# A second merge planned up to 48 gathers earlier, and routing's table lookup in bfloat16

## The reference, cut to what matters

```python
merged = sigmoid(g_a) * (y_a @ w_branch_a) + sigmoid(g_b) * (y_b @ w_branch_b)
h = layer_norm(ALPHA * x + merged @ w_out, ln1_g, ln1_b)
# peer(h): product-key retrieval, 8 heads x top 16 of 128 x 128 experts
q = (h @ w_q).reshape(N, 8, 2, 128)
s = einsum('thcd,chkd->thck', q, sub_keys)           # two half scores of 128 keys
sv, si = top_k(s, 16)
cand = sv[:, :, 0, :, None] + sv[:, :, 1, None, :]   # 16 x 16 candidates
cidx = si[:, :, 0, :, None] * 128 + si[:, :, 1, None, :]
top, j = top_k(cand.reshape(N, 8, 256), 16)
experts = take_along_axis(cidx.reshape(N, 8, 256), j)
gate = softmax(top)
pre = einsum('thkd,td->thk', expert_u[experts], h)
f = einsum('thk,thkd->td', gate * gelu(pre), expert_v[experts])
x = layer_norm(ALPHA * h + f, ln2_g, ln2_b)
```

## Time and profile before

| | |
|---|---|
| median of three runs | 2483.57 us (2473.17 to 2494.70) |
| the profiled execution | 2469.11 us |
| its span, first to last instruction | 2467.3 us |
| mean granted TensorE clock | 0.862 |
| busy share PE, DVE, ACT, POOL | 73%, 58%, 13%, 53% |
| read from memory | 783.86 MB |

### The profile page before, as it was taken

How to read it: one execution, slowest core, us unless ns; L and a number is a source line. 1 busy time by engine, 2 the same in 40 slices (tenths; PEclk the granted TensorE clock), 3 DMA queues, 4 the chain that set the end, 5 groups by cost and what they waited for, 6 DMA issues and landing times. The chain is left out here.

```text
span 2467.3 us, 23559 instructions
## 1 busy us (share of the span) xinstructions
PE 1810.1 (73%) x7247; PEld 762.4 (31%) x7247; DVE 1434.7 (58%) x3191; ACT 309.9 (13%) x737; POOL 1299.2 (53%) x1175
## 2 busy tenths in 40 slices
PE   9999998889779656565576667677778985555466
PEld 6767645645344212111121111221123341110011
DVE  2115875897745843999755669855334447434400
ACT  0214442101010100101010100111010010000000
POOL 1100000467645574545655557767766656767764
PEclk9998987999889888877888889999988996766788
DMA  4206331989979898999999999999999999999997
GB/s 185 71 3 197 95 95 36 336 322 406 409 260 374 290 356 307 402 394 387 392 400 388 402 377 368 370 348 381 393 366 409 409 396 364 376 369 378 354 380 291
DMA packets 259505, 791.67 MB, mean 321 GB/s; under 512 B 31506, under 2 KB 56147, under 8 KB 258803
## 3 DMA queue, kind: packets, MB, share of 16 engines
q0 software_dynamic: 166400, 604.58, 64.3%
q1 hardware_dynamic: 91124, 180.56, 20.8%
q10 hardware_dynamic: 1856, 5.03, 0.5%
HBM read 783.86 MB, written 5.59 MB: 320 GB/s over the span
## 5 line engine op out<-in xcount | busy, mean ns | idle before, releaser
L1319 PE MATMUL ps<-arena 128*32 128x512 f32 x2304 | 790.2, 718 | 346.5 <-DMA arena<-peer_v,arena 295.5
L2001 DVE CUSTOM_DVE_ANT_0 arena<-arena 128x1024 f32<-128x1024 f32 x576 | 695.3, 1226 | 563.5 <-DMA arena<-peer_u,arena 499.7
L895 POOL DMA_INDIRECT arena<-peer_u,arena x576 | 662.0, 1149 | 355.8 <-issue 160.7
L895 POOL DMA_INDIRECT arena<-peer_v,arena x576 | 616.9, 1071 | 393.5 <-PE ps L1319 186.8
L1319 PEld LDWEIGHTS ps<-arena 128*32 128x32 f32 x2304 | 156.7, 122 | 890.3 <-issue 641.3
L1114 PE MATMUL ps<-arena 128*128 128x448 f32 (+2 forms) x512 | 159.2, 472 | 21.3 <-DVE arena L1887 13.2
L1152 PE MATMUL ps<-arena 128*128 128x128 f32 (+2 forms) x768 | 150.4, 354 | 2.3 <-ACT arena L1504 2.3
L1275 PE MATMUL ps<-arena 128*64 128x512 f32 (+1 forms) x512 | 95.5, 516 | 69.3 <-DMA arena<-v_b 66.7
L877 POOL MEMSET arena<- 128x1024 f32 x1 | 1.0, 953 | 274.2 <-ACTq L701 274.2
L927 PE MATMUL ps<-arena 128*128 128x296 f32 (+1 forms) x512 | 130.9, 416 | 6.0 <-DMA arena<-xT 6.0
L1152 PEld LDWEIGHTS ps<-arena 128*128 128x128 f32 x768 | 108.4, 196 | 49.7 <-issue 17.0
(11 more groups left out here) (195 smaller groups left out, 1674.8 us busy)
## 6 DMA issues: line engine op xcount, KB each, us to landing
arena<-k_b SPq DMA_DIRECT2D x128, 256.0 KB
arena<-v_b SPq DMA_DIRECT2D x128, 256.0 KB
arena<-w_mix SPq DMA_DIRECT2D x56, 512.0 KB
arena<-w_q SPq DMA_DIRECT2D x48, 512.0 KB
arena<-kv_a SPq DMA_DIRECT2D x128, 128.0 KB
arena<-w_out SPq DMA_DIRECT2D x24, 512.0 KB
arena<-peer_u,arena POOLq DMA_INDIRECT x576
arena<-peer_v,arena POOLq DMA_INDIRECT x576
```

The costliest lines, as they stand in the source:

```text
L895: pool.indirect_dma_start(out=rows[slot_of[n]], out_offset=None, in_=io["peer_v"] if v else io["peer_u"], in_offset=bass.IndirectOffsetOnA ...
L1319: last = pe.matmul(bank(6 + a, 512, 32 * lane, 32 * lane + 32), strips[:, GT * (G % 2) + k % GT, MID - r_:MID - r_ + 32], rows[slot_of[n]] ...
L2001: dve.tensor_tensor_reduce(out=row, in0=row, in1=h, scale=1.0, scalar=0.0, op0=ALU.mult, op1=ALU.add, accum_out=pre[:, k:k + 1]).then_inc( ...
```

## The change

Three numbers of the plan and its gaps change, tile 1's routes get a running position, and the lookup of step 3 is written anew:

```diff
-        ALONE = 48
+        ALONE = 32
...
             if p:
-                out += [(("mix", p, 0), (0, 10, 6)[p])]
+                out += [(("mix", p, 0), (0, 7, 6)[p])]
                 for m in range(1, KD):
-                    out += [(("mix", p, m), (0, 3, 1)[p]), (("mixed", p, m - 1), (0, 7, 3)[p])]
+                    out += [(("mix", p, m), (0, 2, 1)[p]), (("mixed", p, m - 1), (0, 5, 3)[p])]
                 out += [(("mixed", p, KD - 1), 1)]
-                out += [(("out", p, k), (0, 4, 2)[p]) for k in range(KD)]
+                out += [(("out", p, k), (0, 3, 2)[p]) for k in range(KD)]
...
-                out.append((("query", p, m), (2, 4, 1)[p]))
+                out.append((("query", p, m), (2, 3, 1)[p]))
...
+        at = 0
         for g in range(4):
+            at = max(at, where["score", 1, g] + 2)
             for s_ in range(4):
-                put(where["score", 1, g] + 2 + 3 * s_, "route", 1, g, s_)
+                put(at, "route", 1, g, s_)
+                at += 3
...
-                lagging(dve.tensor_copy(siF[0:nt], si[0:nt]))
-                step(dve.tensor_scalar(jbits[0:nt], tj[0:nt], 4, None, ALU.logical_shift_right))
-                step(dve.tensor_copy(ja[0:nt], jbits[0:nt]))
-                step(dve.tensor_scalar(jbits[0:nt], tj[0:nt], 15, None, ALU.bitwise_and))
-                step(dve.tensor_copy(jb[0:nt], jbits[0:nt]))
-                for c, (jx, ex) in enumerate(((ja, e0), (jb, e1))):
-                    o = oh[0:nt]
-                    o4 = o.rearrange("p (h k) a -> p h k a", h=2)
-                    step(dve.tensor_tensor(o, jx[0:nt].rearrange("p h k -> p (h k)")[:, :, None].to_broadcast([nt, 32, PK]),
-                                           const("iota16", nt)[:, None, :].to_broadcast([nt, 32, PK]), ALU.is_equal))
-                    step(dve.tensor_tensor(o4, o4, siF4[0:nt, :, c, None, :].to_broadcast([nt, 2, PK, PK]), ALU.mult))
-                    step(dve.tensor_reduce(ex[0:nt].rearrange("p h k -> p (h k)"), o, AX_X, ALU.add))
...
+                lagging(dve.tensor_copy(si_b[0:nt], si[0:nt]))
+                for c, (op, by) in enumerate(((ALU.logical_shift_right, 4), (ALU.bitwise_and, 15))):
+                    step(dve.tensor_scalar(jbits[0:nt], tj[0:nt], by, None, op))
+                    step(dve.tensor_copy(j_b[0:nt, c, :], jbits[0:nt].rearrange("p h k -> p (h k)")))
+                o = oh[0:nt]
+                step(dve.tensor_tensor(o, j_b[0:nt, :, :, None].to_broadcast([nt, 2, 32, PK]),
+                                       iota_b[0:nt, None, None, :].to_broadcast([nt, 2, 32, PK]), ALU.is_equal))
+                o5 = o.rearrange("p c (h k) a -> p c h k a", h=2)
+                for c in range(2):
+                    lagging(dve.tensor_tensor(o5[:, c], o5[:, c], si4[0:nt, c, :, None, :].to_broadcast([nt, 2, PK, PK]),
+                                                     ALU.mult))
+                dve.wait_ge(dve_seq, done[0])
+                step(dve.tensor_reduce(e01[0:nt].rearrange("p c n -> p (c n)"), o.rearrange("p c n a -> p (c n) a"), AX_X, ALU.add))
```

More of the change, by code:

```diff
@@ L259, in program @@
         SCB = (0, 1, 2, 0, 1)
-        cand, oh = r.take(2, PK * PK), r.take(32, PK)
+        cand, oh = r.take(2, PK * PK), r.take(512).bitcast(BF16).rearrange("p (c n a) -> p c n a", c=2, a=PK)
         sv = r.take(4, PK)
         si = r.take(4, PK).bitcast(U32)
-        siF = r.take(4, PK)
-        ja, jb, e0, e1 = (r.take(2, PK) for _ in range(4))
+        si_b, j_b = (r.take(2 * PK).bitcast(BF16).rearrange("p (c a) -> p c a", a=n) for n in (PK, 2 * PK))
+        iota_b, e01 = r.take(PK // 2).bitcast(BF16), r.take(2, 2 * PK)
         tj = r.take(2, PK).bitcast(U32)
@@ L1925, in route @@
                 sv4 = sv.rearrange("p (h c) a -> p h c a", c=2)
-                siF4 = siF.rearrange("p (h c) a -> p h c a", c=2)
+                si4 = si_b.rearrange("p (h c) a -> p c h a", c=2)
                 h0, h1 = 2 * g, 2 * g + 2
@@ L1947, in route @@
-                dve.scalar_tensor_tensor(ids[i % 2][0:nt, 32 * g:32 * g + 32], e0[0:nt].rearrange("p h k -> p (h k)"), 128.0,
-                                         e1[0:nt].rearrange("p h k -> p (h k)"), ALU.mult, ALU.add).then_inc(pair_routed, 1)
+                lagging(dve.tensor_copy(si_b[0:nt], si[0:nt]))
+                for c, (op, by) in enumerate(((ALU.logical_shift_right, 4), (ALU.bitwise_and, 15))):
+                    step(dve.tensor_scalar(jbits[0:nt], tj[0:nt], by, None, op))
+                    step(dve.tensor_copy(j_b[0:nt, c, :], jbits[0:nt].rearrange("p h k -> p (h k)")))
@@ L1950, in gate_in @@
+                dve.wait_ge(dve_seq, done[0])
+                step(dve.tensor_reduce(e01[0:nt].rearrange("p c n -> p (c n)"), o.rearrange("p c n a -> p (c n) a"), AX_X, ALU.add))
+                dve.scalar_tensor_tensor(ids[i % 2][0:nt, 32 * g:32 * g + 32], e01[0:nt, 0, :], 128.0, e01[0:nt, 1, :],
+                                         ALU.mult, ALU.add).then_inc(pair_routed, 1)
             def gate_in(i):
@@ L2017, in _ @@
             end_phase(dve, 2)
+            step(dve.tensor_copy(iota_b, const("iota16")))
             for kind, *at in plan:
```

## The result

The median went from 2478.37 us (2463.70 to 2494.70, four executions) to 2534.66 us (2531.34 to 2540.05, four): the ratio is 1.0227, with a 95% interval from 1.0158 to 1.0297. The kernel is slower, by 56 us instead of the 27 that were forecast, and the time lies above the range. The profiled execution took 2540.05 us, 70.9 more than that of before.

The account below looks back on a forecast made before the run. PE was taken to bound the second merge, SP's issues the stage behind it, and DMA the late stretch. Terms -34 + 68 - 6 - 1 = +27 us on a level of 2480.1 gave 2507 us (+1.1%), range 2460 to 2530.

Parts of the forecast that it names:

- the mixes were PE's: Second merge's mixes: PE sets their pace, so they end at about 610 us instead of 617.1.
- the wait at `coef_t`: Tile 0's coefficients in the second merge: PE waits some 13 us for VectorE, a wait the change adds.
- The term of -34: Second merge: its last score comes at about 796 us instead of 829.7, 34 us earlier.
- a gather left for the end costs its full time: Late stretch, where DMA is full: 48 more gathers at 1.42 us each add 68 us.
- The rival that they ride in holes: Late gathers are not the limit, so the merge's 34 us last to the end: about 2440 us; chance 0.15.
- the rival of the long wait at `coef_t`: PE waits 25 us rather than 13 and the mixes give nothing: +49, 2529 us; chance 0.08.
- It stays 114.6: Last score to `ix` of chunk 1: length set by SP's 112.1 us of `kidx` issues, unchanged at 114.6 us.
- I cost this at nothing: SP covers it: Behind the merge: PE reaches `ix` 1 earlier and waits longer for `kidx`, at a cost of 0.
- I take 6 us back, between 0 and 20: Middle, 1500 to 1660 us at 356 GB/s: moved cache loads fill DMA there and save 6 us.
- 1 more for the lookup: Four lookups in tile 3's routes save 3 us of DVE, of which 1 us is taken.
- My last rival: DVE held the mixes: 72 us gained at the merge, balance zero; chance 0.27 together with the paid-back case.
- what the working said: Lookup on DVE: comparison and sum 1.24 us each, two products 0.42 each; 3.3 us, 0.8 saved per lookup.

Follow-up runs that it names:

- before_traced: The kernel before, unchanged, run again for a trace from a chip of the later sets: ratio 1.0015 (0.9998 to 1.0032) against itself.
- the last set: Follow-up runs of the kernel before (1.0015), the changed kernel (1.0087), and a late-routes version with norms four gathers apart and gap 84 (1.0019), against the kernel before.
- after_ctrl3: The changed kernel, unaltered, run and traced once more beside the kernel before: 2444.93 us, ratio 1.0087 (1.0058 to 1.0116).
- plan_only: The kernel before with the new plan, tile 1's routes included, and the old lookup: 2453.78 us, ratio 1.0128 (1.0090 to 1.0165).

## Why the prediction was right or wrong

**Right: the mixes were PE's, in the first result.** I said that no mix could come sooner than PE makes it, about 610 for the end. They ended at 607.9, without a gap. The norm came at 651.7 (654), the first query at 675.2 (677.5), the wait at `coef_t` was 11.71 us (13), the last score at 795.3 (796). The term of -34 measured -34.5.

**Right: a gather left for the end costs its full time.** 48 gathers took 68.7 us, where I had 68. DMA share and pace in the late stretch did not change, 1.43 us each. The rival that they ride in holes fell with that, and so did the rival of the long wait at `coef_t`: it was 12 us, not 25.

**Wrong: the stage behind the merge.** The step that failed says "It stays 114.6", and "I cost this at nothing: SP covers it". It took 128.9 us. I had the right bound, SP's issues, but took their length from one trace as a constant. After, the same 96 issues took 125.2 us. By the starts of the issues, each of the first four dozens took 17 to 24 us, beside 10 to 16 gathers, and the next three 13.4 to 13.7, with 4 gathers and then none. But gathers beside them are not enough to slow them: in `before_traced` the dozens took 13.4 to 13.7 us too, beside 8 to 10 gathers from the second dozen on. This term of 14 us is of the first result alone. In the last set 96 issues took 102.88 us before and 104.56 after, and the stage got 3 us shorter, not 14 longer:

```profile
834.40 102.88 SPq L798 DMA_DIRECT2D arena<-kidx  x96
```

```profile
782.99 104.56 SPq L801 DMA_DIRECT2D arena<-kidx  x96
```

Whether the change or the executions made the difference in the first result is open: it was seen once.

**Wrong: the middle.** The step "I take 6 us back, between 0 and 20", with 1 more for the lookup, had the wrong sign: 7 back was forecast and 22 were lost. This came again in the three later traces of the changed kernel: 13, 20 and 21 us against `before_traced` (in the last set a lead of 54 us at `ix` 1, of 33 at the start of the last 48 gathers). I had looked at one stretch with a low DMA share, and argued that loads moved into it fill it. It did get fuller, 366 GB/s against 356. But I had not asked the same for the stretches that the moved items leave or enter elsewhere: the third merge's mixes lose 11 of the 21 us by the table above. In the first result they lose 6 of the 22 (those 37 gathers took 61.1 us instead of 55.4); where its other 16 went has no cause that is shown. This is the term with the largest error, -7 against +22.

**The size elsewhere.** Of the 44 us that the profiled executions lie above my sum (70.9 against 27), 14 are the stage behind the merge and 29 the middle. The medians give 56 and not 71, since the profiled execution of before lay 9 us under its median, and that of after 5 above.

**What the later sets change.** There the change costs 14 to 27 us, and the sum is made of other terms. My last rival, that VectorE held the mixes of before, was in part true there. PE's mixes of `before_traced`, then of `after_ctrl3`:

```profile
457.05 29.48 PE L1114 MATMUL ps<-arena 128*128 128x448 f32 x80 [0.69 <-ACT arena L1518]
...
492.74 20.05 PE L1114 MATMUL ps<-arena 128*128 128x384 f32 x48 [6.21 <-DVE arena L1887]
...
539.80 77.12 PE L1114 MATMUL ps<-arena 128*128 128x384 f32 x208 [8.45 <-DVE arena L1887]
```

```profile
455.31 137.76 PE L1117 MATMUL ps<-arena 128*128 128x448 f32 x384 [0.69 <-ACT arena L1521]
...
747.80 0.45 PE L1304 MATMUL ps<-arena 128*128 128x128 f32 x1 [10.49 <-DVE arena L1977]
...
884.09 5.26 PE L1189 MATMUL ps<-arena 128*128 128x512 f32 x8 [21.96 <-DMA arena<-kidx]
```

Before, PE could start its mixes at 457 and still ended at 616.9, because it waited for VectorE, 15.8 us over three waits. After, it runs through and ends at 593.1: 24 us gained instead of the 9 of the first result. In the first result PE began 10 and 13 us later (467.0 and 468.6), which the waits of before swallowed and the unbroken row of after did not. So the sum in the last set is: last score -51.4, the stage behind it -3, the middle +21, 48 gathers at 1.28 us +61.4, together the +28.0 of the two spans (2443.9 less 2415.9). The rival had asked for 72 us at the last score and a balance of zero; it got 51, since PE holds the mixes once VectorE does not. And that +28 lies beside my +27 is luck: my terms were -34, 0, -7 and +68. The terms differ by set, and the direction does not: in all four measurements of the changed kernel the interval lies above 1.

**The lookup.** The passes measured what the working said, 1.23 us for the comparison, 0.76 for the two products together and 1.22 for the sum, 3.2 in place of 4.16 us. From DVE's timeline after:

```profile
1151.58 1.23 DVE L1943 TENSOR_TENSOR arena<-arena 128x1024 bf16<-128x1024 bf16 x1
1152.84 0.76 DVE L1947 TENSOR_TENSOR arena<-arena 128x512 bf16<-128x512 bf16 x2
1153.71 1.22 DVE L1950 TENSOR_REDUCE arena<-arena 128x64 f32<-128x1024 bf16 x1
```

Less the fixed 0.15 us that I had worked out from the earlier trace rows, the comparison and the sum take 1.05 ns an element, as the float32 passes did (1.06). The two products take 0.76 us for as many elements. The Trainium skill ("Vector Engine (DVE) Microarchitecture Reference", section 5.1, and "VectorE: DVE Perf Modes", the tier table) gives the first two the rate of one element and the products that of two, and the traces agree. On the kernel's time it showed nothing by itself, with -4 us inside an interval that reaches over 1; that it takes 3 to 16 us off the new plan is suggested by `plan_only` (+30) against the changed kernel (+14 to +27), which ran in other sets.

## What to carry to other kernels

When an item moves up in a plan, ask of each stretch what its own bound engine allows, and price what stays behind at the saturated rate: here 34 to 51 us at the last score were bought with 48 gathers at 1.3 to 1.4 us each. A part that waits on a stream of fixed length (SP's 96 issues) gains nothing from being asked for before the stream is through, and everything queued behind it stands. Moving the merge alone, and leaving what stands behind it in its place, took the loss away and gained nothing that could be measured (0.9986). The 8 us came with the late routes on top. Moving a whole block past others also changes what lies between its items, so look at the waits of every later merge, not only at the stretch with the hole in it.

## What was not expected of the hardware

The same kernel, with the same bytes, had a median of 2478 us in the first result and of 2421 to 2425 us in the four sets. The late stretch shows most of it, gathers and nothing else: 176 in 250 us at 370 GB/s and a share of 0.97 in the first trace, 191 at 410 GB/s and 1.03 in the later one, 1.42 against 1.31 us by the window.

```profile
2150.00:2400.00 250.00, 133.81 (x443) 27.94 (x445) 85.04 (x139) 6.59 (x21) 178.41 (x176) 0.73 0.97 370
```

```profile
2150.00:2400.00 250.00, 150.50 (x529) 34.23 (x531) 84.99 (x139) 6.81 (x22) 182.97 (x191) 0.77 1.03 410
```

The same 96 DMAs of 32 KB were issued by SP in 102.9, 104.6, 112.1 and 125.2 us. Why the chips or the executions differ is not known from these runs.
